# One transformer block pair on one core: projections, sliding attention and delta rule written as one phase, with the l2 norm, the gates, the key swaps and the value scaling moved

## The reference, cut to what matters

```python
u = rmsnorm(h, norm_mix)
proj = u @ w_in                       # aq ak av | dq dk dv dz | db da
attn = sliding_window_sink_attention(rope(aq), rope(ak), av, sinks)
qc, kc, vc = split(silu(causal_conv([dq, dk, dv])))     # 4 heads of 128
qc = l2norm(qc) * 128 ** -0.5;  kc = l2norm(kc)
beta = sigmoid(db);  g = -exp(a_log) * softplus(da + dt_bias)
# chunks: g summed, decay = exp(g_i - g_j), L = strict(k_beta k^T * decay)
T = inverse(I + L);  u = T v_beta;  w = T (k_beta * exp(g))
# scan over chunks with a state of 128 x 128 per head, then norm and silu(dz)
h = h + concat(attn, dn) @ w_o
```

## Time and profile before

| | |
|---|---|
| median of 3 runs | 2287.79 us (2287.36 to 2289.43) |
| profiled execution, its own time | 2286.8 us |
| its span, first to last instruction | 2285.0 us |
| mean granted TensorE clock | 0.941 |
| PE busy | 2025.9 us, 89% |
| PE weight load busy | 1609.6 us, 70% |
| DVE busy | 1325.3 us, 58% |
| ACT busy | 903.0 us, 40% |
| POOL busy | 578.3 us, 25% |
| HBM | 172 GB/s over the span |

### The profile page before, as it was taken

The page is one execution under the profiler, slowest core; times in us unless marked ns, Lnnn a source line. Parts: engine busy times, 40 slices in busy tenths (PEclk is TensorE's granted clock), DMA queues, the critical chain, the costliest instruction groups (busy, mean ns, idle before and its releaser), DMA issues. The chain is left out here.

```text
span 2285.0 us, 24130 instructions
## 1 busy us (share of the span) xinstructions
PE 2025.9 (89%) x8922; PEld 1609.6 (70%) x8922; DVE 1325.3 (58%) x1370; ACT 903.0 (40%) x962; POOL 578.3 (25%) x285
## 2 busy tenths in 40 slices
PE   4998878899999696999998887997899999999991
PEld 3875766688888575767876564885687787777871
DVE  4436664557564257415026253256588888888984
ACT  3104214423223223123001314114678778777862
POOL 2651002100000052524654150650012132212212
PEclk7998889899999797999999898998899999999995
DMA  4221010455552121223224224213499999999983
GB/s 136 94 92 42 21 28 19 159 191 203 176 192 83 55 74 47 90 101 105 98 92 154 86 94 149 92 37 121 148 364 364 362 353 361 358 348 360 372 311 138
DMA packets 175370, 381.16 MB, mean 167 GB/s; under 512 B 21253, under 2 KB 23588, under 8 KB 175166
## 3 DMA queue, kind: packets, MB, share of 16 engines
q1 hardware_dynamic: 161040, 345.80, 42.9%
q10 hardware_dynamic: 8206, 25.28, 3.2%
q0 software_dynamic: 6048, 9.03, 1.1%
HBM read 351.39 MB, written 41.68 MB: 172 GB/s over the span
## 5 line engine op out<-in xcount | busy, mean ns | idle before, releaser
L2606 DVE TENSOR_TENSOR m_lo<-m_raw,m_hi 128x2048 fp32r<-128x2048 f32 x204 | 457.9, 2283 | 8.8 <-ACT m_hi L2546 8.4
L2546 ACT ACTIVATE m_hi<-m_raw 128x2048 fp32r<-128x2048 f32 x204 | 390.3, 1920 | 117.4 <-DMA m_raw<-in_w_exp_gate_dram 82.7
L263 PE MATMUL ps<-xhi,whi 128*128 128x512 f32 x1000 | 398.6, 399 | 31.7 <-DVE xlo L431 12.5
L264 PE MATMUL ps<-xlo,whi 128*128 128x512 f32 x1000 | 393.1, 393 | 0.0
L265 PE MATMUL ps<-xhi,wlo 128*128 128x512 f32 x1000 | 392.6, 393 | 0.0
L240 POOL TENSOR_SCALAR whi<-raw 128x2048 fp32r<-128x2048 f32 (+1 forms) x66 | 124.8, 1891 | 1029.0 <-PE ps L265 1016.2
L242 POOL TENSOR_TENSOR wlo<-raw,whi 128x2048 fp32r<-128x2048 f32 (+1 forms) x66 | 303.1, 4592 | 5.5
L263 PEld LDWEIGHTS ps<-xhi,whi 128*128 128x128 f32 x1000 | 189.9, 190 | 84.5 <-issue 32.3
L263 PE MATMUL ps<-m_hi,xt_hi 128*128 128x512 f32 x544 | 219.7, 404 | 24.0 <-DVE xt_lo L2611 16.0
L265 PEld LDWEIGHTS ps<-xhi,wlo 128*128 128x128 f32 x1000 | 190.1, 190 | 40.3
L264 PEld LDWEIGHTS ps<-xlo,whi 128*128 128x128 f32 x1000 | 190.4, 190 | 39.8 <-issue 1.5
(11 more groups left out here) (438 smaller groups left out, 3089.6 us busy)
## 6 DMA issues: line engine op xcount, KB each, us to landing
m_raw<-in_w_exp_gate_dram SPq DMA_DIRECT2D x68, 1024.0 KB, 7.3
m_raw<-in_w_exp_up_dram SPq DMA_DIRECT2D x68, 1024.0 KB, 7.3
m_raw<-in_w_exp_down_dram SPq DMA_DIRECT2D x68, 1024.0 KB, 6.9
raw<-in_w_in_dram SPq DMA_DIRECT2D x42, 1024.0 KB, 5.2
ada_w<-in_w_ada_dram ACTq DMA_DIRECT2D x48, 512.0 KB, 4.1
y_rows<-hT SPq DMA_DIRECT2D x39, 512.0 KB, 5.1
raw<-in_w_up_dram SPq DMA_DIRECT2D x16, 1024.0 KB, 5.7
raw<-in_w_down_dram SPq DMA_DIRECT2D x16, 1024.0 KB, 5.0
```

The source lines that it names most:

```text
L263: nc.tensor.matmul(o, lh, rh, start=start, stop=False)
L264: nc.tensor.matmul(o, lh, rl, start=False, stop=False)
L2546: nc.scalar.activation(m_hi[s][:], m_raw[s][:], ACT.Copy).then_inc(m_split, 1)
L2606: nc.vector.tensor_tensor(m_lo[s][:], m_raw[s][:], m_hi[s][:].bitcast(F32), ALU.subtract).then_inc(m_low, 1)
```

## The change

The three phases become one: no meeting of the engines at the two seams. Inside it:

- The eight sums of the l2 norm go in pairs through banks 0 and 1 between the products of the key and value unit; ScalarE takes the four logarithms and two exponentials there, and VectorE its eight products before the rotations.
- The first gate operations on VectorE stand before the key and value copies, ScalarE's part before SiLU of z, the last four on VectorE after the eight products.
- The key swap of group 0 stands inside the second half of z, after its second tile; that of group 1 directly after z.
- SyncE issues the small loads of phases two and three early.
- The last attention tile's turn and low part stand inside the start of the delta rule. The rows of decays use banks 0 to 3, betas banks 4 and 5, key products banks 6 and 7, each with its own order of waits.
- The scaling of the value and key-end tiles (`v_beta`, `k_end`) is done by ScalarE, one activation per head with a scale per partition, 32 in all. All four chunks' `items` stand before the substitution. The attention output tiles stand behind all items.
- ScalarE's queue issues the eight transfers into `inv_t`. GpSimd clears `inv_a` and `inv_t` once the last value product is done and splits no output-projection chunk until the scan has begun.

```diff
+                def sums(r):
+                    if r >= 2:
+                        pe.wait_ge(l2_inv, r // 2)
+                    for b in range(2):
+                        nc.tensor.matmul(ps[:, b, :], ones, l2_t[:, r + b, :], start=True, stop=True).then_inc(l2_sum, 1)
+                sums(0)
...
+                def swap_key(g):
+                    pe.wait_ge(rope_mul, 4 * g + 4)
+                    nc.tensor.matmul(ps[:, 5 + 2 * g, :], dup[:, 2 * g, :], k_raw[:], start=True, stop=True)
+                    nc.tensor.matmul(ps[:, 4 + 2 * g, :], dup[:, 2 * g + 1, :], k_raw[:], start=True, stop=True).then_inc(rope_pe, 1)
+                pe.wait_ge(kv_out, 2)
+                pe.wait_ge(l2_inv, 4)
+                linear(pe, U_dz, (xhi, xlo), between=swaps, inside=((4, 1), lambda: swap_key(0)))
+                swap_key(1)
...
             @block.gpsimd
             def _(pool):
+                stream_split(pool, PHASE["win"])
+
+                pool.wait_ge(value_pe, len(AU))
                 nc.gpsimd.memset(inv_a[:], 0.0).then_inc(zeroed, 1)
                 nc.gpsimd.memset(inv_t[:], 0.0).then_inc(zeroed, 1)
+                pool.wait_ge(scan_new, 1)
                 stream_split(pool, PHASE["wo"])
...
                 rows(0)
+                turn_out(len(AU) - 1)
+                rows(1)
                 betas(0)
-                rows(1)
-                keys(0)
                 betas(1)
                 rows(2)
+                rows(3)
+                keys(0)
                 keys(1)
                 betas(2)
-                rows(3)
+                betas(3)
                 keys(2)
-                betas(3)
                 keys(3)
-                linear_tile(pe, U_wa[0], (xhi, xlo), 0)
-                items(0)
-                linear_tile(pe, U_wa[0], (xhi, xlo), 1)
-                items(1)
-                linear_tile(pe, U_wa[0], (xhi, xlo), 2)
-                linear_tile(pe, U_wa[0], (xhi, xlo), 3)
-                items(2)
-                items(3)
+                for c in range(TT):
+                    items(c)
+                for m in range(4):
+                    attention_tile(0, m)
                 for m in range(2):
-                    linear_tile(pe, U_wa[1], (xhi, xlo), m)
+                    attention_tile(1, m)
...
+                act.wait_ge(end_act, 1)
+                for c in range(TT):
+                    for i, (dst, col) in enumerate(((v_beta, beta[:, c, :]), (k_end, g_col[:, 2, c]))):
+                        n = 3 * c + 1 + i
+                        act.wait_ge(item_pe, n + 1)
+                        for h in range(GH):
+                            ins = nc.scalar.activation(dst[:, c, h], heads(4 + n % 4)[:, h], ACT.Identity, scale=col[:, h:h + 1])
+                        ins.then_inc(item_act, 1)
+                act.wait_ge(zeroed, 2)
+                act.wait_ge(i_out, 32)
+                blocks_back(act, 0, inv_t, i_in_t)
...
+                for r in range(8):
+                    dve.wait_ge(l2_inv, 5 + r // 4)
+                    nc.vector.scalar_tensor_tensor(delta_in[:, r, :], delta_in[:, r, :], P ** -0.5 if r < 4 else 1.0, l2_t[:, r, :],
+                                                   ALU.mult, ALU.mult).then_inc(l2_done, 1)
...
-                items(0)
-                items(1)
+                for c in range(TT):
+                    items(c)
                 dve.wait_ge(l_in, 16 * NB)
...
-                items(2)
-                items(3)
+                residual(dve, U_wa[0], 0)
```

More of the change, by code:

```diff
@@ L302, in linear @@
                         last.then_inc(lin_full, 1)
+                    if inside is not None and inside[0] == (k0, m):
+                        inside[1]()
                 if n != mine[-1]:
@@ L1008, in _ @@
             def _(pe):
+                for i, u in enumerate(U_dn):
+                    linear(pe, u, (xhi, xlo), ready=(x_ready, 0) if i == 0 else None)
+                linear(pe, U_aq, (xhi, xlo))
+                pe.wait_ge(ba_split, 2)
+                pe.wait_ge(lin_free[side(U_dn[2])], 4 * (nth(U_dn[2]) + 1))
+                for kk in range(KT):
+                    last = three(ps[0:8, 3, :], wba_hi[:, kk, :], wba_lo[:, kk, :], xhi[:, kk, :], xlo[:, kk, :],
+                                 kk == 0, kk == KT - 1)
@@ new lines, in turn_out @@
+                def turn_out(i):
+                    pe.wait_ge(*out_dve.at("norm", i))
+                    if i >= 1:
+                        pe.wait_ge(att_lo, i)
+                    for a in range(2):
+                        last = nc.tensor.transpose(att_turned(i)[:, a], att_o[:, i % 2, 2 * a:2 * a + 2, :].rearrange("p j n -> p (j n)"), ident)
+                    last.then_inc(out_turn, 1)
+                pe.wait_ge(key_pad, 1)
+                pe.wait_ge(rope_done, TT + AKV)
+                scores(0)
@@ new lines, in _ @@
+                for m in range(4):
+                    act.wait_ge(lin_full, 4 * U_aq + m + 1)
+                    nc.scalar.activation(qT[:, m, :], bank(U_aq, m), ACT.Copy).then_inc(lin_free[side(U_aq)], 1)
+                for r in range(0, 8, 2):
+                    act.wait_ge(l2_sum, r + 2)
+                    nc.scalar.activation(l2_t[:, r:r + 2, :], ps[:, 0:2, :], ACT.Ln, bias=eps_col).then_inc(l2_inv, 1)
+                for half in (0, 4):
+                    act.wait_ge(l2_inv, 4)
+                    nc.scalar.activation(l2_t[:, half:half + 4, :], l2_t[:, half:half + 4, :], ACT.Exp,
+                                         scale=-0.5).then_inc(l2_inv, 1)
@@ new lines, in _, with exps @@
+                for m in range(4):
+                    act.wait_ge(lin_full, 4 * U_dz + m + 1)
+                    nc.scalar.activation(delta_in[:, 12 + m, :], bank(U_dz, m), ACT.Silu).then_inc(lin_free[side(U_dz)], 1)
+                def exps(i):
+                    v = att_v[:, i % 2]
+                    act.wait_ge(*soft.at("shift", i))
+                    nc.scalar.activation(att_s[:, i % 2], att_s[:, i % 2], ACT.Exp).then_inc(soft_act.sem, 1)
+                    act.wait_ge(*soft.at("gap", i))
+                    nc.scalar.activation(v[:, 8:12], v[:, 4:8], ACT.Exp).then_inc(soft_act.sem, 1)
@@ new lines, in high @@
+                def high(i):
+                    act.wait_ge(out_turn, i + 1)
+                    nc.scalar.activation(att_slot(xhi, i), att_turned(i), ACT.Copy).then_inc(att_hi, 1)
+                exps(0)
+                for i in range(len(AU)):
+                    for half in range(2):
+                        act.wait_ge(turn_pe, 2 * i + half + 1)
+                        if i >= 2:
+                            act.wait_ge(value_pe, i - 1)
+                        nc.scalar.activation(att_t[:, i % 2, 4 * half:4 * half + 4, :],
+                                             ps[:, 4 + half, :].rearrange("p (a n) -> p a n", n=P), ACT.Copy).then_inc(turn_act, 1)
+                    if i >= 1:
+                        high(i - 1)
+                    if i + 1 < len(AU):
+                        exps(i + 1)
@@ new lines, in _ @@
+                dve.wait_ge(gate_act, 4)
+                own(4, nc.vector.tensor_tensor(pos, pos, gate_t[:, 4], ALU.add))
+                own(5, nc.vector.scalar_tensor_tensor(step[:], pos.rearrange("p (t h) -> p t h", h=GH), -1.0,
+                                                      a_log[:].unsqueeze(1).to_broadcast([P, TT, GH]), ALU.mult, ALU.mult))
+                own(6, nc.vector.tensor_scalar(gate_t[:, 5], gate_t[:, 5], 1.0, None, ALU.add))
+                own(7, nc.vector.reciprocal(beta[:], gate_t[:, 5].rearrange("p (t h) -> p t h", h=GH)))
```

595 lines of the change are left out of this document (245 added, 350 removed).

## The result

The changed kernel takes 2257.17 us, the median of 4 runs (2251.66 to 2261.53); the kernel before took 2288.61 beside it on the same chip (4 runs). The ratio is 0.9861, 95% interval 0.9838 to 0.9884: 1.2 to 1.6% less time. The forecast was 2263.8 with a range of 2255 to 2276. Six more executions of the same code, taken with the experiments, have a median of 2264.1 (2255.98 to 2266.97; ratio 0.9900, 0.9883 to 0.9917).

What follows compares the result with a forecast made beforehand. TensorE's products were taken to bound the projections, VectorE attention and the delta front; terms sum to a first level step 24.0 us earlier, 2286.8 to 2262.8, plus 1.0 for the median: 2263.8 us, range 2255 to 2276.

Steps and rivals of the forecast that it cites:

- mask: Start of attention: first mask 8.0 us later, at 199.5, with VectorE's SBUF-only work waiting behind GpSimd's splits.
- first unit: Attention, first mask to end of first value product: 11.6 us instead of 15.6, 4.0 shorter, at half clock.
- later units (l2 products): Attention up to the last value product: 41.6 us, bound by VectorE, loses eight l2 products, 5.0 us.
- last value product to `lower`: Seam and delta front: last `lower` 13.7 us after the last value product against 21.1, 7.4 less.
- `lower` to substitution: Delta rule's items: twelve TensorE steps at 0.9 us, 10.8 in all; this term gains 0.3 us.
- substitution: Substitution in the delta rule: 9.1 us instead of 14.6, 5.5 less, since GpSimd's split waits for the scan.
- turned copy to level step: From the substitution's copy to the first level step: 7.5 us instead of 17.3, 9.8 less.
- rival A: VectorE stays longer behind GpSimd and attention sees half clock twice: gain 14 to 19, about 2271 us; chance 0.2.
- Rival C: TensorE at half clock from last value product to first level step: slower, ending at 2302 us; chance 0.05.
- rival D: The blocks' transfers set the substitution anyway, landing 3 to 5 us later: gain 19 to 21, 2268; chance 0.1.
- Scales: ScalarE's 32 scales in the items: 1.1 us per tile, hidden; VectorE is spared 4.8 us.
- Level step: First level step at 288.5 us: residual addition done at 288.4, inverse transfer landed at 288.0.

Runs made afterwards that it cites:

- same_as_after: The changed kernel again, unaltered, for six more executions; median 2264.1 us, ratio 0.9900 to the kernel before.
- splits_after_values: The changed kernel with GpSimd's splits of both first chunks of the attention output's weights moved behind the last value product; 2253.2 us, ratio 0.9854 to the kernel before.
- l2_in_units: The changed kernel with the eight l2 products back inside the softmax units; 2266.5 us, ratio 0.9915 to the kernel before.
- splits_after_filled: splits_after_values with dummy products added in TensorE's idle gaps (two before attention, four in the second unit, one in the last); 2251.9 us, ratio 0.9847.
- blocks_shared: splits_after_filled with the inv_a block transfers put first and shared by SyncE's and ScalarE's queues, inv_t's following on both; 2245.3 us, ratio 0.9817.
- splits_late: The changed kernel with GpSimd's first two output-chunk splits held until the last gate operation and the last key rotation; 2260.0 us, ratio 0.9878.
- filled_gaps: The changed kernel with ten dummy products in TensorE's idle gaps around the first scores and in the last unit; 2249.5 us, ratio 0.9845.

## Why the prediction was right, and where it was not

The forecast was 24.0 us less; the profiled executions differ by 25.3, and by 25.2 up to the last VectorE operation. That nearness is in part chance. Of the 25.2, only 19.2 come from the stretch of the change; 2.1 come from the level step to the stage of the difference norms, 3.5 from that stage (153.8 us instead of 157.3, at clock 0.92 instead of 0.90) and 0.5 from behind it, all in code that did not change and that the forecast put at nothing. The second execution has the stretch at 26.4. The forecast lies between the two, and both medians of the code, 2257.2 and 2264.1, lie in its range.

By its own terms, against both executions of the changed kernel:

| term | forecast | after | same_as_after |
|---|---|---|---|
| mask | +8.0 | +7.4 | +7.8 |
| first unit | -4.0 | -4.1 | -4.1 |
| later units (l2 products) | -5.0 | +1.1 | -4.8 |
| last value product to `lower` | -7.4 | -5.6 | -7.5 |
| `lower` to substitution | -0.3 | -2.4 | -2.5 |
| substitution | -5.5 | -5.4 | -5.4 |
| turned copy to level step | -9.8 | -10.0 | -9.9 |
| sum | -24.0 | -19.2 | -26.4 |

- *Mask.* Size right and mechanism right: VectorE's work of two SBUF operands behind GpSimd's splits. splits_after_values moves two of the splits away and gets 6.6 back. The operations that waited were partly others than I named: one of the l2 products, but also two gate operations on 16 columns at 4.43 and 4.45, a third at 1.90 beside a split's high part, and no query rotation. z's last tile came at 189.5 for 188, by the swap's wait.
- *First unit.* 11.5 from the mask to the end of the first value product for the 11.6 worked out, at half clock as assumed.
- *Later units.* The eight products at 5.0 are about right (4.1 for seven in l2_in_units). The 41.6 that I took them from was not bound by VectorE alone: the kernel before had its sixth unit at half clock, which I did not read, and it made the way from the third mask to the eighth 0.7 longer than in l2_in_units:

```profile
233.96 3.67 PE L792 MATMUL ps<-v_tok,att_t 128*128 128x65 f32 x16 [0.52 <-ACT att_t L900]
```

 In the profiled execution after, a second unit and the last one at half clock took 5.9 back against same_as_after. Such a spell was named, in rival A and as "another spell at half clock 2 to 3 more", and counted at nothing in the sum. It is the step that failed for that execution.
- *Seam and front.* 13.5 in same_as_after, 13.7 forecast. With the last unit at half clock, the front begins at half clock too (0.58) and takes 15.4. The reason that I gave for full clock, that TensorE comes busy out of attention, does not hold in that execution. Rival C, half clock up to the level step, did not happen: the clock was 1.00 from 258 us on in both.
- *Items.* Mis-sized by 2.1 (0.3 forecast, 2.4 measured): I priced the twelve steps alike at 0.9. Two steps of three are transposes, and they cost half. On TensorE's timeline after, one row of x8 is four heads' products, the next of x8 eight transposes, two steps:

```profile
267.50 1.06 PE L868 MATMUL ps<-delta_in 128*128 128x128 f32 x8
268.40 1.04 PE L870 MATMUL ps<-cbase,delta_in 128*128 128x128 f32 x8
```

so 7.7 us instead of 10.8 (267.5 to 275.2). With the items that much earlier, the wait for the blocks (rival D) came close to deciding; where it did decide it was 0.7 us at most, in splits_after_filled.
- *Scales.* 1.0 to 1.1 per tile against my 1.1; hidden, and worth what VectorE is spared, 4.6.
- *Substitution.* 9.2 long for 9.1, 9.6 with the turned copy, and no step over 0.56. The split in the scan cost nothing, as put.
- *Level step.* Both conditions lay within 1 us of each other in the forecast, and blocks_shared showed that they do.

Two large terms, the moved items and the split, are not independent: once the items stand ahead, the split without its wait misses the substitution and costs 1.9 to 3.4 us, not 5.5.

Open remains what was not undone by itself: the two seams, the order of the items, the eight sums and the key swaps in their new places. Their shares are read from dates, and no run separates them.

## To carry to other kernels

When phases are fused, list for each engine pair what the new order puts side by side: here GpSimd's splits met VectorE's SBUF-only work and cost 6.6 us at the first mask until two of them were moved beside PSUM work. Read TensorE's clock behind each idle gap (2.2 to 5.6 us here): ten dummy products brought the level step to 280.5, the best new place of the splits to 282.5, both together to 277.1, and the held-back splits, which left a gap of 5.23 us behind, gave their gain back. Judge an edit of a few us by the date at which its stretch ends, with the clock beside it and in more than one execution: the rest of this kernel varied by 11 us, the stretch itself by 7, and most dates above stand on a single execution.

## What the runs showed of the hardware

- Small VectorE operations are held by GpSimd like large ones: one on 16 columns (128x16) from one SBUF tile and a constant took 4.45 us, one on four columns 2.68. Operations with one operand in PSUM were not held beside two whole splits (244 to 255 us in splits_after_values; the 1.1 and 0.7 us operations keep their lengths). The Trainium skill, "SBUF — State Buffer", "SBUF: two separate sides", has VectorE and GpSimd take one port pair by turns for a whole instruction, with two SBUF inputs or in a two-port mode; the trace agrees.
- A long duration is not always a wait. Beside GpSimd's clear in splits_after_filled VectorE's rows read

```profile
252.21 2.08 DVE L1245 COPY g_col<-work_b 128x4 f32<-128x4 f32 x1
252.28 2.01 DVE L1246 TENSOR_TENSOR kbg<-kbg,work_b 128x512 f32<-128x512 f32 x1
252.88 1.41 DVE L1247 TENSOR_TENSOR delta_in<-delta_in,work_b 128x512 f32<-128x512 f32 x1
253.48 0.81 DVE L1243 TENSOR_TENSOR a_qk<-ps,work_a 128x512 f32<-128x512 f32 x1
```

 and all end at 254.29, with the clear, yet they start 0.60 apart, their usual pitch: nothing was delayed. Why the records are long stays open. The clears, put at nothing in the forecast, show no cost here.
- TensorE was at half clock behind idle gaps of 3.3 to 5.6 us, and behind one of 2.15 us too (first scores of splits_late, 3.67 us long); with 1.3 us ahead of the first scores and at most 0.8 us in the first two units it stayed at 1.00 (filled_gaps). The Trainium skill, "TensorE: Matmul & The Clock Gate", Part 1, has idleness as the cause; the trace agrees. Whether half clock came back in the second and in the last unit (gap 1.22 us) differed between executions of the same code; what decides that stays open.
- The stage of the difference norms took 152.0 to 155.4 us in five of the executions and 157.3 to 157.8 in the others, and the rest behind it 876.6 to 886.5, with no edit there.
